# First mixer: items three in flight, operands of 31 and 36 rows padded to 128, gate folded into the scaling, output begun in the last items, gate slot moved

## The chip, the cores and the metric

The kernel runs on one core of a Trainium2 chip. Its metric is the device time of one execution in microseconds (us); lower is better. The core has five engines with queues of their own that work in parallel and wait for each other on semaphores: TensorE (PE: matmuls and transposes into PSUM banks), VectorE (DVE), ScalarE (ACT), GpSimd (POOL) and SyncE (SP, which issues the weight loads).

## The reference

The program is a chain of transformer blocks on 512 tokens of width 1024, in float32. The change touches only the mixer of the first block, whose heart is this:

```python
def _even_mixer(h, w_in, ...):
    aq, ak, av, ao, ai, af, bq, bkc, bvc, bks, bvs, bkw, bvw, bg = _split(h @ w_in, EVEN_SIZES)
    ya = _mlstm(aq, ak, av, ao, ai + a_i_b, af + a_f_b, a_conv, a_norm)
    yb = _nsa(bq, bkc, bvc, bks, bvs, bkw, bvw, bg + b_g_b, b_cmp_pos, b_cmp_w1, b_cmp_w2)
    return jnp.concatenate([ya, yb], -1) @ w_out

# _nsa, for each block of queries, head pair and branch (compressed, selected, window)
    p = _masked_softmax(s, mask)          # s = q k^T; 31 compressed keys, or up to 512
    o = gb[..., 0:1] * o_cmp + gb[..., 1:2] * o_sel + gb[..., 2:3] * o_win

# _mlstm, for each of 4 heads (gates ig, fg; written here over all 512 tokens at once)
    S = (q k^T) * exp(D - m);  hc = (S v) / max(|den|, exp(-m))
    hn = (hs - mean) * rsqrt(var + eps) * norm_g;  ya = hn * sigmoid(o)
```

`_mlstm` is the "memory" part, `_nsa` the "heads" part. Behind the mixer come a residual with layer norm, an MLP and the other blocks, which the change leaves alone.

## The kernel before

Every weight is float32 and is used as a high and a low half. SP loads a slot (up to 128 x 2048) into one of two raw buffers; ScalarE writes the high half (L1293, whi); the low half, raw minus high, is written by GpSimd (L3119, wlo) or VectorE (L2047). A product is three matmuls: whi with the high half of x, wlo with it, whi with x's low half (L591 to L593, `mm3`). There are two pairs of halves: a slot's pair can be written only when the slot two before it has been used. The order of slots is written out in `weight_plan`: e_in (four slots of 256 columns), e_g (96 columns: the gates of both parts), e_vs, the two compressions with e_qk, two more e_qk, e_vo (four) and e_out (eight half slots, four for each half of the columns). All engines' programs go through it in that order.

In the first stage (to about 134 us of the span) TensorE makes the projections. From the gate product, VectorE and ScalarE work out the memory part's row vectors (`r_ls`, `r_b`, `r_M`: bias, Abs, Exp, +1, Ln, two scans; ScalarE L1521 to L1527, VectorE L2385 to L2404), and the window sums for the compression (`windows`, L2374) are VectorE's too. ScalarE's copy `hw` into an_e (L1482 in the records, which is the line of the copy helper) and a transpose of it follow.

From about 134 to 365 us runs a loop over 48 items. An item is a block of 128 queries (q, 0 to 3), two key groups (g), two head pairs (j) and a branch (br: 0 compressed with 31 keys, 1 selected, 2 window with (q + 1) x 128 keys). Its steps are:
- `first`: scores on TensorE (L914 to L916 for br 0, L918 to L920 otherwise), row maxima on VectorE (L2531), exp with row sum on ScalarE (L1617)
- `scaled`, on VectorE: reciprocal of the sums (L2538), times the gate (L2542), for q = 0 and br = 0 times a row mask (L2545), then P times that (L2549), for each of two heads
- `second`: transposes of P on TensorE (L933), the copy to PT on VectorE for odd items (L2292), on ScalarE for even ones (L1482)
- `third`: product with the values (L948; operand vc of 31 rows for br 0, vsw of 128 rows otherwise), and after br 2 the copy to yb (L2576), or for q = 3 its split into xh and xl (ScalarE L1641, VectorE L2572)

Round n of the loop does `first(n)`, one unit of the memory part, `second(n - 1)` and `third(n - 2)` on every engine; on VectorE `scaled(n)` stands behind the unit. From item 12 on every third round does a second unit. P and PT have two copies each, by n % 2. The units are, in order, the rest of e_qk and the e_vo products; for each of four heads four decay units (scores L864, decay with nmr and sel of 36 rows L867, VectorE L2468) and four value units (L877, denominator L1586, L2475, L2477, scaling L2479); then statistics (L2486, L2490), norms (L2500), and transposes of the memory output (L611, copied by L2114). The last unit splits yb of the first three query blocks (L2511). Behind the loop TensorE waits for all of this and begins the output, e_out (L591 again).

Of the kernel before, what the change touches and what calls it, by code (L numbers as in the profile page):

```python
# [7 lines left out]
F = mybir.dt.float32  # L8
# [300 lines left out]
def weight_plan(I):  # L309
# [21 lines left out]
    add_fm("e_in", v, 0, 1024)  # L331
    plan.slot("e_g", v[:, :, 3328:3424])
    add_fm("e_vs", v, 1024, 1280)
# [66 lines left out]
def memory(nc, k):  # L400
# [19 lines left out]
    def even():  # L420
        with ExitStack() as sc:
# [9 lines left out]
            s.gts, s.nmr, s.gcol = tmp("gts", [128, NT, 24]), tmp("nmr", [36, T], R), tmp("gcol", [128, 2, NT, 4])  # L431
            s.sel, s.vc = tmp("sel", [36, 512], R), tmp("vc", [32, 2, 2, 64])
# [5 lines left out]
            s.P, s.PT, s.PT_e = tmp("P", [128, 4, T]), tmp("PT", [128, 4, T]), tmp("PTe", [128, 1280])  # L438
# [5 lines left out]
            s.blk = [x[:, 0:2, :].rearrange("p a (l g m) -> p (a l) g m", l=8, g=2) for x in (s.P, s.PT)]  # L444
# [132 lines left out]
def tensor_program(nc, k):  # L577
# [212 lines left out]
    def even():  # L790
        e = k.even
        fm("e_in", [[("e_in", 2 * n), ("e_in", 2 * n + 1)] for n in range(4)], x, need=lambda kk: ("x", kk))
        pe.wait_ge(at("con"))
# [7 lines left out]
        slots.done()  # L801

# [48 lines left out]
        def memory():  # L851
# [8 lines left out]
            for hh in range(4):  # L860
# [11 lines left out]
                for q in range(NT):  # L872
                    pe.wait_ge(at("PT_e", hh, 3))
# [7 lines left out]
            yield  # L881
            yield
# [6 lines left out]
            yield  # L889
# [33 lines left out]
        def second(n):  # L923
# [3 lines left out]
            for z in range(0, nk, 256):  # L927
                bank = take(("at", n, z))
                for i, kk in enumerate(range(z, min(z + 256, nk), 128)):
                    w = min(128, nk - kk)  # L930
                    for h in range(2):
                        o = i * 256 + h * 128
                        ins = M.transpose(bank[0:w, o:o + 128], e.P[:, (n % 2) * 2 + h, kk:kk + w], ident)  # L933
                ins.then_inc(*made.inc(("made", ("at", n, z)), ("P turned", n)))

        def third(n):
# [7 lines left out]
            for kk in range(0, nk, 128):  # L944
                w = min(128, nk - kk)
                lhs = e.vc[0:31, g, :, :] if br == 0 else e.vsw[:, kk // 128, br - 1, g, :, :]
                rhs = e.PT[0:w, (n % 2) * 2 + kk // 256, kk % 256 * 2:kk % 256 * 2 + 256]
# [5 lines left out]
        for n in range(N + 2):  # L953
# [15 lines left out]
        ho.next("ln")
        tm("e_out", ("e_out",), 0, D, x, early=True, after=residual)  # L970
# [2462 lines left out]
```

## Time and profile before

| | us |
| --- | --- |
| three runs | 3425.53, 3427.07, 3427.49 (median 3427.07) |
| the profiled execution, own time | 3425.47 |
| its span | 3424.2 |
| TensorE busy | 3264.3 (95%) |
| VectorE busy | 2040.2 (60%) |
| ScalarE busy | 1458.4 (43%) |
| GpSimd busy | 915.4 (27%) |

The profile is of one execution. Times in rows are from the span's start. PEld is the weight load of TensorE, which overlaps the matmuls; the ends of matmuls are modelled, so for TensorE the distance from start to start says more than the durations. The granted clock is a share of full speed: 1.00 is 2.4 GHz and 0.50 is 1.2 GHz. What stands in brackets behind a row is the engine's idle time ahead of it and what ended that.

### The profile page before, as it was taken

How to read it: one execution, taken by the hardware profiler on the slowest of the kernel's cores; microseconds unless marked ns; L12 is line 12 of the kernel's file. 1: busy time of each engine (PE TensorE's matmuls, PEld its weight loads, DVE VectorE, ACT ScalarE, POOL GpSimd, SP SyncE). 2: the span in 40 equal slices, each digit the busy share in tenths (PEclk: the TensorE clock that was granted, in tenths of full speed). 3: DMA queues.
4: the chain of work that ended last, by engine and by line, in shares of the span. 5: the costliest groups of instructions: out<-in, count | busy, mean ns of one | idle time of the engine just before them, and what ended most of it. 6: DMA issues, size and time to landing. Idle time of an engine off the chain costs nothing.

```text
span 3424.2 us, 47853 instructions
## 1 busy us (share of the span) xinstructions
PE 3264.3 (95%) x20089; PEld 2885.8 (84%) x20092; DVE 2040.2 (60%) x3066; ACT 1458.4 (43%) x2246; POOL 915.4 (27%) x415
## 2 busy tenths in 40 slices
PE   8898999999879999999999999999999999999998
PEld 6786789988667899979899878999999998789998
DVE  4557555464683644567556635755785566367556
ACT  4454345453432544445334323543453343235433
POOL 3120024321421233311233231223222332312232
PEclk9999999999999999999999999999999999999999
DMA  3310323331112233222332323233323323232232
GB/s 129 102 50 1 111 74 118 105 105 60 52 43 74 82 106 121 93 86 69 123 105 87 111 74 99 84 90 111 111 74 117 105 87 111 74 99 94 90 107 75
DMA packets 239815, 308.97 MB, mean 90 GB/s; under 512 B 8337, under 2 KB 168097, under 8 KB 239089
## 3 DMA queue, kind: packets, MB, share of 16 engines
q1 hardware_dynamic: 236016, 291.41, 26.4%
q0 software_dynamic: 3584, 14.52, 1.2%
q8 instruction: 158, 2.59, 0.3%
q14 instruction: 57, 0.46, 0.0%
HBM read 303.80 MB, written 2.10 MB: 89 GB/s over the span
## 4 chain that ended last, share of the span: by engine, by line
PE 73%; DVE 21%; ACT 4%; issue 2%; DMA 0%; POOL 0%; DVEq 0%; ACTq 0%
PE bank L591 23%; PE bank L593 23%; PE bank L592 23%; DVE wlo L2041 3%; ACT whi L1293 1%; DVE wraw L2063 1%; DVE raw_w L2063 1%; DVE xl L2114 1%; DVE wkk_o L2865 1%; ACT P_e L1617 1%; DVE gb L2862 1%; DVE uv_x L2995 1%; DVE ul_w L2241 1%; DVE P_e L2549 1%; PE bank L1232 1%
## 5 line engine op out<-in xcount | busy, mean ns | idle before, releaser
L3119 POOL TENSOR_TENSOR wlo<-wraw,whi 128x1024 fp32r<-128x1024 f32 (+4 forms) x219 | 565.8, 2587 | 1606.4 <-ACT whi L1293 1605.9
L591 PE MATMUL bank<-xh,whi 128*128 128x256 f32 (+1 forms) x2456 | 722.9, 294 | 48.7 <-DVE zt L2236 21.0
L1293 ACT ACTIVATE whi<-wraw 128x1024 fp32r<-128x1024 f32 (+3 forms) x426 | 440.5, 1038 | 693.7 <-PE bank L593 553.9
L593 PE MATMUL bank<-xh,wlo 128*128 128x256 f32 (+1 forms) x2456 | 717.9, 292 | 0.0
L592 PE MATMUL bank<-xl,whi 128*128 128x256 f32 (+1 forms) x2456 | 714.0, 291 | 0.0
L591 PEld LDWEIGHTS bank<-xh,whi 128*128 128x128 f32 x2456 | 466.2, 190 | 69.4 <-issue 27.6
L3119 POOL TENSOR_TENSOR wlo<-raw_w,whi 128x1024 fp32r<-128x1024 f32 (+1 forms) x130 | 310.1, 2388 | 724.6 <-ACT whi L1293 724.6
L592 PEld LDWEIGHTS bank<-xl,whi 128*128 128x128 f32 x2456 | 466.3, 190 | 10.4
L593 PEld LDWEIGHTS bank<-xh,wlo 128*128 128x128 f32 x2456 | 465.2, 189 | 10.6
L591 PE MATMUL bank<-whi,uh_w 128*128 128x512 f32 x1216 | 473.8, 390 | 0.0
L593 PE MATMUL bank<-whi,ul_w 128*128 128x512 f32 x1216 | 473.3, 389 | 0.0
L592 PE MATMUL bank<-wlo,uh_w 128*128 128x512 f32 x1216 | 473.2, 389 | 0.0
L1293 ACT ACTIVATE whi<-raw_w 128x1024 fp32r<-128x1024 f32 (+1 forms) x315 | 307.8, 979 | 362.3 <-PE bank L593 263.1
L2041 DVE TENSOR_TENSOR wlo<-wraw,whi 128x1024 fp32r<-128x1024 f32 (+1 forms) x207 | 239.8, 1161 | 315.6 <-ACT whi L1293 314.8
L591 PE MATMUL bank<-whi,xh 128*128 128x512 f32 (+2 forms) x976 | 375.7, 385 | 9.0 <-POOL wlo L3119 3.6
L591 PE MATMUL bank<-ah_w,whi 128*128 128x256 f32 x1296 | 367.4, 284 | 10.7 <-DVE wraw L2063 6.8
L592 PE MATMUL bank<-wlo,xh 128*128 128x512 f32 (+2 forms) x976 | 369.8, 379 | 0.0
L593 PE MATMUL bank<-whi,xl 128*128 128x512 f32 (+2 forms) x976 | 369.7, 379 | 0.0
L592 PE MATMUL bank<-al_w,whi 128*128 128x256 f32 x1296 | 366.6, 283 | 0.0
L593 PE MATMUL bank<-ah_w,wlo 128*128 128x256 f32 x1296 | 366.5, 283 | 0.0
L2041 DVE TENSOR_TENSOR wlo<-raw_w,whi 128x1024 fp32r<-128x1024 f32 (+1 forms) x185 | 211.8, 1147 | 253.7 <-ACT whi L1293 252.9
L593 PEld LDWEIGHTS bank<-whi,ul_w 128*128 128x128 f32 x1216 | 228.2, 188 | 48.0
(401 smaller groups left out, 5085.8 us busy)
## 6 DMA issues: line engine op xcount, KB each, us to landing
wraw<-in_w_in SPq DMA_DIRECT2D x26, 1024.0 KB, 5.3
wraw<-in_ffn_w_down SPq DMA_DIRECT2D x20, 1024.0 KB, 5.1
raw_w<-in_ffn_w_down SPq DMA_DIRECT2D x20, 1024.0 KB, 5.1
raw_w<-in_mlp_w SPq DMA_DIRECT2D x19, 1024.0 KB, 5.1
wraw<-in_mlp_w SPq DMA_DIRECT2D x17, 1024.0 KB, 5.1
wraw<-in_ffn_w_gate SPq DMA_DIRECT2D x32, 512.0 KB, 5.1
raw_w<-in_ffn_w_gate SPq DMA_DIRECT2D x32, 512.0 KB, 4.9
raw_w<-in_ffn_w_up SPq DMA_DIRECT2D x32, 512.0 KB, 4.5
```

Source lines behind the costliest of these rows:

```text
L591: M.matmul(o, lh, rh, start=start, stop=False, skip_group_check=more)
L592: M.matmul(o, lh, rl, start=False, stop=False, skip_group_check=more)
L593: return M.matmul(o, ll, rh, start=False, stop=stop, skip_group_check=more)
L1232: i = M.matmul(bank[:, q * 128:(q + 1) * 128], s.PT[:, hh % 2, o:o + 128], s.vt[:, t, hh * 128:(hh + 1) * 128], start=(t == 0), stop=(t == q))
L1293: A.activation(hi, raw, ACT.Copy).then_inc(*k.w_hi.inc(("hi", j)))
L1617: A.activation(e.P[:, (n % 2) * 2 + h, 0:nk], ring.of(key)[:, 0:nk], ACT.Exp, bias=m, accum_out=e.rsum[:, n % 4, h:h + 1]).then_inc(*done. ...
L2041: V.tensor_tensor(lo, raw, hi.bitcast(F), ALU.subtract).then_inc(*k.w_lov.inc(("lo", j)))
L2063: V.tensor_tensor(b, x, y, ALU.subtract).then_inc(*done.inc(("sum of", j)))
L2114: V.tensor_tensor(lo, ring.of((*key, f))[:, :].rearrange("p (f t) -> p f t", f=4), hi.bitcast(F), ALU.subtract).then_inc(*done.inc((*name, ...
L2241: V.tensor_tensor(quarter(s.ul, u, c, a), t.rearrange("p (f t) -> p f t", t=256), quarter(s.uh, u, c, a).bitcast(F), ALU.subtract).then_in ...
L2549: V.tensor_scalar(p, p, c[:, hf:hf + 1], None, ALU.mult).then_inc(*done.inc(("P scaled", n)))
L3119: G.tensor_tensor(lo[:, 0:n], raw[:, 0:n], hi[:, 0:n].bitcast(F), ALU.subtract).then_inc(*k.w_lo.inc(("lo", j)))
```

## The change

It has six parts, all in the first mixer.
1. The gates' slot e_g goes ahead of the last e_in slot, and the row vectors' chain with it on each engine: on VectorE ahead of the last slot's copies, on ScalarE Abs and Exp ahead of them and Ln between them.
2. The loop has one more item in flight: `scaled(n - 1)`, `second(n - 2)`, `third(n - 3)`, N + 3 rounds, P and PT split by branch in place of n % 2. On VectorE `scaled(n - 1)` stands ahead of the unit for items 0 and 1 and behind it from item 2 on. The second unit comes from item 9 on.
3. vc, PT of branch 0, nmr and sel have 128 rows, the added ones zero.
4. The gate is the second pointer operand of L2549's successor; the multiply L2542 goes, and the row mask is applied once to the first gates.
5. Statistics are made in each value unit; value unit q waits for decay unit q only, and the denominator's max takes its second operand as a pointer. There are 61 units where there were 64.
6. The first half of the rows' products of output column 0 (`out_first`, 12 matmuls for each token tile) for tiles 0 and 1 is made in the last two units, for tiles 2 and 3 right behind the loop; `out_second` follows, and then the second half of the columns. The split of yb moves behind the loop on VectorE, and to round N on ScalarE.

```diff
-    add_fm("e_in", v, 0, 1024)
+    add_fm("e_in", v, 0, 768)
     plan.slot("e_g", v[:, :, 3328:3424])
+    add_fm("e_in", v, 768, 1024)
...
-            s.gts, s.nmr, s.gcol = tmp("gts", [128, NT, 24]), tmp("nmr", [36, T], R), tmp("gcol", [128, 2, NT, 4])
-            s.sel, s.vc = tmp("sel", [36, 512], R), tmp("vc", [32, 2, 2, 64])
+            s.gts, s.nmr, s.gcol = tmp("gts", [128, NT, 24]), tmp("nmr", [128, T], R), tmp("gcol", [128, 2, NT, 4])
+            s.sel, s.vc = tmp("sel", [128, 512], R), tmp("vc", [128, 2, 2, 64])
...
-            s.P, s.PT, s.PT_e = tmp("P", [128, 4, T]), tmp("PT", [128, 4, T]), tmp("PTe", [128, 1280])
+            s.P, s.PT, s.PT_e = tmp("P", [128, 2112]), tmp("PT", [128, 2304]), tmp("PTe", [128, 1280])
...
+            s.p_of = [(s.P[:, a:a + w], s.P[:, a + w:a + 2 * w]) for a, w in ((0, 32), (64, 512), (1088, 512))]
+            s.pt_of = [s.PT[:, a:a + w] for a, w in ((0, 256), (256, 1024), (1280, 1024))]
...
# TensorE
...
-        fm("e_in", [[("e_in", 2 * n), ("e_in", 2 * n + 1)] for n in range(4)], x, need=lambda kk: ("x", kk))
-        pe.wait_ge(at("con"))
+        fm("e_in", [[("e_in", 2 * n), ("e_in", 2 * n + 1)] for n in range(3)], x, need=lambda kk: ("x", kk))
...
+        fm("e_in", [[("e_in", 6), ("e_in", 7)]], x)
+        pe.wait_ge(at("con"))
...
-                    pe.wait_ge(at("PT_e", hh, 3))
+                    pe.wait_ge(at("PT_e", hh, q))
...
+                if q > 1:
+                    out_first(q - 2)
...
+        def out_first(tt):
+
+            key = ("e_out", 0, tt)
+            pe.wait_ge(at("og turned", tt))
+            bank = take(key, True)
+            for p, kr in enumerate(k_items(8)[0:2]):
+                tm_part(slots.get("e_out", p), kr, bank, key, tt, x, 8, None, 512, last=tt == NT - 1)
+
+        def out_second():
+            slots.done(2)
+            for kr in k_items(8)[2:4]:
+                j = slots.get("e_out")
+                for tt in range(NT):
+                    key = ("e_out", 0, tt)
+                    if tt < NT - 1:
+                        pe.wait_ge(at("yb split"))
+                    else:
+                        pe.wait_ge(at("yb split 3"))
+                    tm_part(j, kr, ring.of(key), key, tt, x, 8, None, 512, last=tt == NT - 1)
+                    if kr[1] == 8:
+                        ring.drop(key)
+                slots.done()
 
         pe.wait_ge(at("cmb"))
...
-                lhs = e.vc[0:31, g, :, :] if br == 0 else e.vsw[:, kk // 128, br - 1, g, :, :]
-                rhs = e.PT[0:w, (n % 2) * 2 + kk // 256, kk % 256 * 2:kk % 256 * 2 + 256]
+                lhs = e.vc[:, g, :, :] if br == 0 else e.vsw[:, kk // 128, br - 1, g, :, :]
+                rhs = e.pt_of[br][:, kk * 2:kk * 2 + 256]
...
-        for n in range(N + 2):
+        for n in range(N + 3):
             if n < N:
                 first(n)
             next(units, None)
-            if n >= 12 and n % 3 == 0:
+            if n >= 9 and n % 3 == 0:
                 next(units, None)
-            if 0 <= n - 1 < N:
-                second(n - 1)
             if 0 <= n - 2 < N:
-                third(n - 2)
+                second(n - 2)
+            if 0 <= n - 3 < N:
+                third(n - 3)
         run(units)
         made.so_far(("end", "even", "pe"))
...
+        out_first(2)
+        out_first(3)
+        out_second()
+        tm("e_out", ("e_out",), 512, D, x, early=True, after=residual)
...
# ScalarE
...
+        def e_in_ln(key):
+            e_in(key)
+            if key[1] == 6:
+                act.wait_ge(at("r_ls one"))
+                A.activation(e.r_ls, e.r_ls, ACT.Ln).then_inc(*done.inc(("r_ls ln",)))
+        fm("e_in", [[("e_in", 6), ("e_in", 7)]], e_in_ln)
+        act.wait_ge(at("con"))
+        act.wait_ge(at("eps"))
+        def e_vs(key, tt):
+            copy_out(key, e.vsw[:, tt, :, :, 0, :], ring.of(key)[:, 0:256].rearrange("p (a g d) -> p a g d", a=2, g=2), ("vsw one", tt))
+        run(tm_units("e_vs", ("e_vs",), e_vs))
         act.wait_ge(at("r_bM"))
...
+            if n == N:
+                act.wait_ge(at("yb one", 35))
+                act.wait_ge(at("yb", 35))
+                A.activation(xh[:, 4:8, 0:384], e.yb[:, :, 0:384], ACT.Copy).then_inc(*done.inc(("yb hi",)))
...
# VectorE
...
+        V.memset(e.vc[:, :, :, :], 0.0).then_inc(*done.inc(("vc empty",)))
...
-        fm("e_in", [[("e_in", 6), ("e_in", 7)]], e_in)
-        windows(1)
...
+        windows(1)
...
+        fm("e_in", [[("e_in", 6), ("e_in", 7)]], e_in)
...
+        first_gate = e.gts[:, 0, :].rearrange("p (h j) -> p h j", j=3)[:, :, 0]
+        V.tensor_scalar(first_gate, first_gate, con[:, C_ROW:C_ROW + 1], None, ALU.mult).then_inc(*done.inc(("gts masked",)))
+        dve.wait_ge(at("gts masked"))
...
-                    V.tensor_tensor(d, d, e.gcol[:, 1, q, hh:hh + 1], ALU.max).then_inc(*done.inc())
+                    V.tensor_scalar(d, d, e.gcol[:, 1, q, hh:hh + 1], None, ALU.max).then_inc(*done.inc())
                     dve.wait_ge(done.now())
...
-                    yield
-            for q in range(NT):
-                for hh in range(4):
-                    j = q * 4 + hh
                     dve.wait_ge(at("hs", hh, q))
                     V.bn_stats(st[:, j, 0, :], e.hs[:, q, hh, :]).then_inc(*done.inc())
-                dve.wait_ge(done.now())
-                for hh in range(4):
-                    j = q * 4 + hh
+                    dve.wait_ge(done.now())
...
-            V.reciprocal(c, c).then_inc(*done.inc())
             h0 = 4 * g + 2 * j
             gate = e.gts[:, q, :].rearrange("p (h j) -> p h j", j=3)[:, h0:h0 + 2, br]
+            V.reciprocal(c, c).then_inc(*done.inc())
             dve.wait_ge(done.now())
-            V.tensor_tensor(c, c, gate, ALU.mult).then_inc(*done.inc())
-            dve.wait_ge(done.now())
-            if br == 0 and q == 0:
-                V.tensor_scalar(c, c, con[:, C_ROW:C_ROW + 1], None, ALU.mult).then_inc(*done.inc())
-                dve.wait_ge(done.now())
             for hf in range(2):
-                p = e.P[:, (n % 2) * 2 + hf, 0:nk]
-                V.tensor_scalar(p, p, c[:, hf:hf + 1], None, ALU.mult).then_inc(*done.inc(("P scaled", n)))
+                p = e.p_of[br][hf][:, 0:nk]
+                V.tensor_scalar(p, p, c[:, hf:hf + 1], gate[:, hf:hf + 1], ALU.mult, ALU.mult).then_inc(*done.inc(("P scaled", n)))
 
         def second(n):
...
-        for n in range(N + 2):
+        for n in range(N + 3):
             if n < N:
                 first(n)
+            if 0 <= n - 1 < 2:
+                scaled(n - 1)
             next(units, None)
-            if n < N:
-                scaled(n)
-            if n >= 12 and n % 3 == 0:
+            if 2 <= n - 1 < N:
+                scaled(n - 1)
+            if n >= 9 and n % 3 == 0:
                 next(units, None)
-            if 0 <= n - 1 < N:
-                second(n - 1)
             if 0 <= n - 2 < N:
-                third(n - 2)
+                second(n - 2)
+            if 0 <= n - 3 < N:
+                third(n - 3)
         run(units)
+        dve.wait_ge(at("yb hi"))
+        hi, lo = xh[:, 4:8, 0:384], xl[:, 4:8, 0:384]
+        V.tensor_tensor(lo, e.yb[:, :, 0:384], hi.bitcast(F), ALU.subtract).then_inc(*done.inc(("yb split",)))
         barrier("even")
         enter()
         ho.next("ln")
```

In ScalarE's program the waits for buffers go from the item two before to the item three before, and its loop changes as TensorE's does.

## Rows read from the trace of the kernel before

**Rows 1.** page, section 4: the chain that ended last, share of the span by engine
```profile
PE 73%; DVE 21%; ACT 4%; issue 2%; DMA 0%; POOL 0%; DVEq 0%; ACTq 0%
```

**Rows 2.** windows, five stretches of the first mixer; columns as in the first line
```profile
core 0: us, PE busy (x) PEld busy (x) DVE busy (x) ACT busy (x) POOL busy (x), PEclk, DMA share, GB/s
65.50:110.00 44.50, 35.26 (x226) 31.56 (x226) 27.25 (x32) 17.13 (x22) 11.24 (x7) 0.92 0.24 79
155.70:219.70 64.00, 63.79 (x498) 60.72 (x497) 28.99 (x98) 40.62 (x96) 14.11 (x4) 0.96 0.18 58
219.70:300.10 80.40, 72.77 (x409) 52.53 (x407) 54.41 (x194) 36.78 (x132) 4.87 (x2) 0.96 0.04 14
300.10:364.90 64.80, 50.77 (x267) 38.41 (x267) 50.87 (x166) 27.95 (x81) 0.77 (x1) 0.89 0.09 33
364.90:410.00 45.10, 45.10 (x202) 36.61 (x203) 19.91 (x27) 10.82 (x15) 5.84 (x4) 1.00 0.36 117
```

**Rows 3.** windows, for the granted clock (PEclk), four stretches; same columns
```profile
95.90:99.30 3.40, 3.40 (x13) 2.80 (x12) 0.20 (x2) 1.35 (x2) 0.00 (x0) 0.51 0.00 0
154.00:160.00 6.00, 6.00 (x25) 5.02 (x26) 2.57 (x14) 4.92 (x12) 0.00 (x0) 0.50 0.50 167
322.85:341.85 19.00, 13.18 (x55) 9.72 (x54) 15.89 (x56) 9.63 (x24) 0.00 (x0) 0.73 0.00 0
250.95:300.10 49.15, 44.84 (x264) 32.61 (x263) 34.36 (x122) 21.83 (x82) 0.00 (x0) 1.00 0.00 1
```

**Rows 4.** timeline of TensorE: start us, us, instruction [idle before <-releaser]
```profile
69.19 0.58 PE L591 MATMUL bank<-whi,xh 128*128 128x256 f32 x1 [3.65 <-POOL wlo L3119]
...
95.37 0.27 PE L825 MATMUL bank<-con,an_e 64*128 64x64 f32 x1 [3.50 <-ACT an_e L1482]
...
153.97 0.69 PE L933 MATMUL bank<-con,P_e 128*128 128x128 f32 x2 [3.48 <-DVE P_e L2549]
```

**Rows 5.** timeline of ScalarE and GpSimd around the gate slot
```profile
48.84 0.60 ACT L1482 ACTIVATE kvT_e<-bank 128x512 f32<-128x512 f32 x1 [5.00 <-PE bank L593]
...
64.37 4.77 POOL L3119 TENSOR_TENSOR wlo<-wraw,whi 128x2048 fp32r<-128x2048 f32 x1 [12.08 <-ACT whi L1293]
...
91.51 0.63 ACT L1527 ACTIVATE gb<-og_e 4x512 f32<-4x512 f32 x1 [4.60 <-DVE og_e L2404]
```

**Rows 6.** timeline of ScalarE behind the exp of item 2
```profile
156.28 0.63 ACT L1537 ACTIVATE qk_e<-PTe_e 128x512 f32<-128x512 f32 x1
```

**Rows 7.** waits in 219.7 to 364.9: total us, times, longest
```profile
ACT P_e L1617 <- DVE nm_e L2531: 73.1, 32, 3.6
DVE PTe_e L2468 <- ACT kvT_e L1482: 14.5, 12, 1.4
...
DVE den_e L2475 <- ACT den_e L1586: 9.8, 12, 1.0
```

**Rows 8.** timeline of TensorE, an item's last product and the next item's first
```profile
165.76 0.60 PE L948 MATMUL bank<-PT_e,vsw_e 128*128 128x256 f32 x2
166.01 0.41 PE L918 MATMUL bank<-kh_e,qs_e 128*128 128x128 f32 x1
...
169.94 0.69 PE L948 MATMUL bank<-PT_e,vc_e 31*128 31x256 f32 x2
170.56 0.28 PE L914 MATMUL bank<-kch_e,qs_e 128*128 128x32 f32 x1
```

**Rows 9.** VectorE by form, from 130 or 219.7 on: count, busy us, mean ns, idle
```profile
L2549 DVE TENSOR_SCALAR P_e<-P_e,rsum_e 128x128 f32<-128x128 f32 x16 | 3.9, 283 | 0.3
...
L2542 DVE TENSOR_TENSOR rsum_e<-rsum_e,gts_e 128x2 f32<-128x2 f32 x33 | 5.3, 161 | 1.1
...
L2500 DVE TENSOR_SCALAR qk_e<-qk_e,mv,rs 128x128 f32<-128x128 f32 x16 | 4.4, 342 | 0.1
...
L2486 DVE BATCH_NORM_STATS2 st<-qk_e 128x6 f32<-128x128 f32 x16 | 3.4, 277 | 0.0
...
L2490 DVE BATCH_NORM_AGGREGATE mv<-st 128x2 f32<-128x6 f32 x16 | 1.5, 158 | 0.1
```

More of the change, by code:

```diff
@@ L880, in memory @@
             yield
-            yield
-            yield
             for q in range(NT):
@@ L1505, in e_in @@
                     A.activation(e.kh[other, i - 6, g, :], src, ACT.Copy).then_inc(*done.inc(("ks hi twice", i - 6, g)))
-        fm("e_in", [[("e_in", 2 * n), ("e_in", 2 * n + 1)] for n in range(4)], e_in)
-        act.wait_ge(at("con"))
-        act.wait_ge(at("eps"))
+        fm("e_in", [[("e_in", 2 * n), ("e_in", 2 * n + 1)] for n in range(3)], e_in)
         slots.get("e_g")
@@ L1516, in even @@
         A.activation(e.r_f, bank[64:68, :], ACT.Copy).then_inc(*done.inc(("r_f",), ("free", ("e_g",))))
-        def e_vs(key, tt):
-            copy_out(key, e.vsw[:, tt, :, :, 0, :], ring.of(key)[:, 0:256].rearrange("p (a g d) -> p a g d", a=2, g=2), ("vsw one", tt))
-        run(tm_units("e_vs", ("e_vs",), e_vs))
+        slots.prepare()
         act.wait_ge(at("r_f bias"))
@@ L1523, in even @@
         A.activation(e.r_ls, e.r_ls, ACT.Exp, scale=-1.0).then_inc(*done.inc(("r_ls exp",)))
-        act.wait_ge(at("r_ls one"))
-        A.activation(e.r_ls, e.r_ls, ACT.Ln).then_inc(*done.inc(("r_ls ln",)))
+        def e_in_ln(key):
[9 more added lines that the diff above has]
+        run(tm_units("e_vs", ("e_vs",), e_vs))
         act.wait_ge(at("r_bM"))
@@ L1597, in memory @@
                 yield
-            act.wait_ge(at("yb one", 35))
-            act.wait_ge(at("yb", 35))
-            A.activation(xh[:, 4:8, 0:384], e.yb[:, :, 0:384], ACT.Copy).then_inc(*done.inc(("yb hi",)))
-            yield
         units = memory()
@@ L2354, in even @@
         V.tensor_copy(k.idb[:, :], k.ident)
-        V.tensor_copy(e.sel[:, :], con[0:36, C_SEL:C_SEL + 512]).then_inc(*done.inc(("sel",)))
+        V.tensor_copy(e.sel[:, :], con[:, C_SEL:C_SEL + 512]).then_inc(*done.inc(("sel",)))
         V.memset(e.nmr[:, :].bitcast(F), 0.0).then_inc(*done.inc(("nmr empty",)))
@@ L2508, in memory @@
                 yield
-            dve.wait_ge(at("yb hi"))
-            hi, lo = xh[:, 4:8, 0:384], xl[:, 4:8, 0:384]
-            V.tensor_tensor(lo, e.yb[:, :, 0:384], hi.bitcast(F), ALU.subtract).then_inc(*done.inc(("yb split",)))
-            yield
         units = memory()
@@ L2518, in even @@
         dve.wait_ge(at("made", key))
+        dve.wait_ge(at("vc empty"))
         V.tensor_copy(e.vc[0:31, :, 0, :], src)
@@ L2576, in third @@
                 V.tensor_copy(e.yb[64:128, f, s], o[64:128, 128:256]).then_inc(*done.inc(("yb", n), ("free", key)))
-        for n in range(N + 2):
+        for n in range(N + 3):
             if n < N:
                 first(n)
+            if 0 <= n - 1 < 2:
+                scaled(n - 1)
             next(units, None)
-            if n < N:
-                scaled(n)
-            if n >= 12 and n % 3 == 0:
+            if 2 <= n - 1 < N:
+                scaled(n - 1)
+            if n >= 9 and n % 3 == 0:
                 next(units, None)
-            if 0 <= n - 1 < N:
-                second(n - 1)
             if 0 <= n - 2 < N:
-                third(n - 2)
+                second(n - 2)
+            if 0 <= n - 3 < N:
+                third(n - 3)
         run(units)
+        dve.wait_ge(at("yb hi"))
+        hi, lo = xh[:, 4:8, 0:384], xl[:, 4:8, 0:384]
+        V.tensor_tensor(lo, e.yb[:, :, 0:384], hi.bitcast(F), ALU.subtract).then_inc(*done.inc(("yb split",)))
         barrier("even")
@@ L3167, in even @@
         G.dma_start(e.w2, I["w2"]).then_inc(*k.landed["w2"].inc(("w2",)))
-        slots.skip("e_in", 4)
+        slots.skip("e_in", 3)
         slots.skip("e_g", 1)
+        slots.skip("e_in", 1)
         slots.get("e_vs")
```

33 lines of the change are left out of this document (11 added, 22 removed).

## The prediction

> **What bounds the kernel now.** I began with the chain that ended last [rows 1]: 73% of it runs on TensorE, and of the rest most on VectorE. So time can be taken out only where TensorE waits or is slow. The table of stretches [rows 2] says where, in the first mixer: in 65.5 to 110 TensorE is busy 35.26 of 44.5 us; in 155.7 to 219.7 it is full (63.79 of 64); in 219.7 to 300.1 it is busy 72.77 of 80.4; in 300.1 to 364.9 only 50.77 of 64.8; in 364.9 to 410 it is full again, 202 matmuls in 45.1 us, 0.223 us each. These five stretches have different limits, and the change touches all of them. The granted clock [rows 3] is at its lower level (1.2 GHz, shown as 0.50) for the 3.4 us from 95.9 and in 154 to 160, both times right behind a wait of 3.5 us [rows 4]. TensorE's waits there are 3.65 us for a weight's low half from GpSimd (at 69.19), 3.50 us for ScalarE's hw (L1482, out an_e), and 3.48 us for item 0's scaled P. A stretch of 3.4 us at half clock costs 1.7 us where TensorE is the limit.
>
> In 219.7 to 364.9 the waits [rows 7] read otherwise: ScalarE's exp waits 73.1 us for the row maxima of VectorE, and VectorE waits 14.5 + 9.8 = 24.3 us for ScalarE in its memory units (decay and denominator). TensorE and GpSimd set little there: the bound is a loop, VectorE max, ScalarE exp, ScalarE unit, VectorE unit, VectorE scaling, next max.
>
> **A, gate slot moved (base 48.8 us).** Now the e_g product ends at 65.5 and the gate rows are the first thing behind it, with the next high part just before; its low half on GpSimd takes 4.77 us [rows 5], so TensorE waits 3.65 us, and 1.7 more go at half clock. After the change the last e_in slot, 48 matmuls, lies between the gate product and e_vs, so the split of e_vs and the gate chain, which ends with ScalarE's L1527 at 91.51 [rows 5], have 11 us more. That removes 3.65 + 1.7 and 3.50 + 1.7 = 10.55 us. In return the last e_in slot's own pair can be split only when the slot two before it is used, at 48.8. With some 2 us for the high half (an estimate, under half of GpSimd's 4.77 for the same size) behind the copy that starts at 48.84, and 4.77 for the low half, it is ready at about 56.0. The gate product, 24 matmuls of 0.223, started at 48.8 ends at 54.2. So a new wait of 1.8 us. Sum -8.7. Bounds: the new wait may grow to 3.5 with a fall of the clock (-5.5), or vanish (-10.5). The gate chain is queued on VectorE ahead of the last two e_in copies and the window sums; it holds the low half of the next DVE-split slot, which I price at 0 to 2.
>
> **B, three in flight, items 0 to 3.** TensorE stands at 153.97 for P of item 0 [rows 4]. A lag of one more item asks for it later; scaling of items 0 and 1 stays ahead of the unit. But what then comes next is PT(0), copied by ScalarE behind its table load and a silu that ends at 156.9 [rows 6]: about 157.0, against third(0)'s 154.59 now. So only part of 3.48 + 1.7 us goes: -2.5 (0 to -4.5).
>
> **C, padding.** The trace has the same product with 128 rows and 31 rows [rows 8]: from start to next start it is 0.25 us with 128 (165.76 to 166.01) and 0.62 with 31 (169.94 to 170.56): 0.37 us per such item. Five of the 16 fall where TensorE is full (items 3 to 15), -1.9; the extra unit from item 9 on moves work into it, +0.8. Sum -1.1 (-3 to +1). In the rest TensorE has slack, and padding nets nothing there. A rule speaks against it: the Trainium skill, page "TensorE: Matmul & The Clock Gate", section "Why this matters for your kernels", says that a single K=32 matmul takes the same time as K=128, with which the padding would gain 0 and C would be +0.8. The trace disagrees with 0.25 against 0.62.
>
> **D, items 16 to 35, VectorE's loop.** Per item the gate multiply (L2542) goes: 0.161 plus 0.035 of spacing, 0.196. The scaling gets a second pointer: L2500 (two) at 128x128 took 342 ns, L2549 (one) 283 [rows 9]; +0.057 each, two per item, +0.11. Net -0.085 x 20 = -1.7. The statistics move into the value units: 0.277 + 0.158, with one more signal wait between them and one for hs 0.52 (an estimate), and the max with a pointer +0.07. Twelve of the 16 units lie here (the other four begin after 305): 12 x 0.59 = +7.1. Unit shift, -0.5. Sum +4.9 (+2 to +7). The depth doesn't take the 24.3 us of waits for ScalarE, in my reading: after the change the scaling of the item before stands behind the unit, the unit waits for ScalarE's unit, and this for exp(n) and that for max(n); the loop stays closed.
>
> **E, item 36 to the output's first matmul, 64.8 us.** Out go 16 statistics and 16 aggregates in four batches, 1.20 each, -4.8; in come four inline at 0.6, +2.4; scaling -0.085 x 12 = -1.0; the last wait for the yb split -1.0, as the two output tiles left stand ahead of it; one more lap in flight at the end, +1.7. Sum -2.7. And two first halves of output tiles, 24 matmuls, are done inside, where TensorE idles 14 of 64.8 us: 24 x 0.223 [rows 2] = -5.4. The clock is 0.89 there; more work in it could be at half speed, +0.8. Sum -7.3 (-11 to -2). Weights for both e_out slots are on the chip before, since DMA moves little there (33 GB/s, [rows 2]).
>
> **Sum.** -8.7 - 2.5 - 1.1 + 4.9 - 7.3 = -14.7 on the profiled execution's 3425.47 (its span is 3424.2, 1.3 less), 3410.8; the median shown is 1.6 higher, so 3412 us. What follows (the output stage and the MLP) is bound by TensorE at 45.1 of 45.1, so the gain carries through to the end. Of the moved slot everything moves: its load on SP's queue changes place with the last e_in slot's, its high half on ScalarE's and its low half on GpSimd's. No wait of TensorE there is for a load [rows 4], and DMA is busy 0.24 of the stretch behind, so I price the loads at nothing; without that cover one slot's load would be in question.
>
> **Rivals.** Four cases, the main one being the sum above.
>
> R2: the depth does open the loop. ScalarE's exp no longer feeds the scaling in its own round, and were the 24.3 us of waits in VectorE's units gone for half or more, with D at -9 instead of +4.9, the sum is -29, 3398. For: the waits, 24.3 us in all, are the largest of VectorE's [rows 7]. Against: the order of the unit ahead of the scaling.
>
> R3: only the small parts count. New wait of A with a fallen clock and the low half queued behind the gate chain (-4), B nothing, E -4, D +5: -5, 3422.
>
> R4, on the other side: the clock. In 322.85 to 341.85 TensorE is busy 13.18 of 19 us and the clock is 0.73 [rows 3]: where it works in short bursts between waits, it is slow part of the time. In 250.95 to 300.1 it is busy 44.84 of 49.15 us at clock 1.00. Should the changed order of bursts bring the lower level there too, at a mean clock of 0.60 its work takes 44.84 / 0.60 = 74.7 us, and TensorE takes the bound over: +25.6 on the sum of the others, -14.7, gives 3438. It decides, slower by more than 6.9 us, once the clock's mean there falls below 0.63, where 44.84 us of work become 71. For: padding and the moved unit shorten TensorE's work in the same loop, so it idles a larger share. Against: the change takes 0.37 us of matmul from every third item there, of 44.84 in all, and the stretch now holds 1.00. The Trainium skill, page "TensorE: Matmul & The Clock Gate", section "A second HAM failure mode: psum-queue depth-cycling", describes a kernel whose engine idled briefly between groups of matmuls and so kept falling back; the trace agrees for 322.85 to 341.85 (0.73), while 250.95 to 300.1 has waits too and stays at 1.00.
>
> **How the numbers follow.** Main case 0.62, its own range -24 to -6 (3403 to 3421), from the bounds above taken partly together; R2 0.17; R3 0.12; R4 0.09. A measurement of this kernel can tell 0.2%, 6.9 us, from no change. Most of R3 (0.10) and a tenth of the main case (0.06) lie within it: 0.16. Slower is R4 but for a little, 0.08. Faster is the rest, 0.76. The range to leave out no more than 2 in 10: 3396 to 3424, the upper end the small case, the lower end the open loop.
>
> **What would show it.** After: no wait of over 2 us for GpSimd or hw between 50 and 110, one of about 1.8 at the slot behind the gates (A); no L948 with 31 rows, and about 0.25 us from it to the next first (C); L2549 at 0.34 for 128 columns and 0.56 for 512 (D); VectorE still waiting some 20 us for ScalarE's kvT and den between items 16 and 35 (against R2); the clock above 0.9 there (against R4); 24 matmuls of the output ahead of the last third (E). It is wrong if the loop in D opens, if ScalarE, which the moved Exp and Ln give other table loads, becomes late in A, or if a stall in another place lowers the clock.

## The result and the profile after

The changed kernel took 3414.23 us (median of 6 runs, 3413.44 to 3415.14), the kernel before 3426.34 us (6 runs): a ratio of 0.9963, 95% interval 0.9951 to 0.9974, so 12.1 us less where the forecast had 14.7. The profiled execution took 3413.44 us, its span 3412.1.

The windows of the changed kernel, cut where item 0, item 4, item 16 and item 36 begin, where the output begins behind the loop, and where the MLP's first product begins (columns as in [rows 2]):

```profile
126.20:149.20 23.00, 20.61 (x128) 17.85 (x126) 14.60 (x32) 17.40 (x27) 6.87 (x2) 0.99 0.29 92
149.20:208.80 59.60, 58.23 (x463) 55.82 (x462) 26.21 (x73) 39.30 (x94) 13.92 (x4) 0.98 0.17 54
208.80:293.70 84.90, 68.14 (x397) 53.92 (x395) 59.63 (x194) 37.61 (x129) 4.66 (x2) 0.92 0.04 13
293.70:357.80 64.10, 51.85 (x307) 40.99 (x306) 48.09 (x134) 28.77 (x84) 0.77 (x1) 1.00 0.10 33
357.80:399.00 41.20, 41.20 (x187) 33.45 (x186) 23.80 (x32) 11.88 (x17) 5.82 (x4) 1.00 0.40 132
```

The same points in both traces, from the starts of TensorE's instructions, give the balance by stage:

| to | before, at us | after, at us | this stage | forecast |
| --- | --- | --- | --- | --- |
| item 0 | 134.35 | 126.23 | -8.1 | A -8.7 |
| item 4 | 161.9 | 149.2 | -4.6 | B -2.5 |
| item 16 | 219.7 | 208.8 | +1.8 | C -1.1 |
| item 36 | 298.1 | 293.7 | +6.5 | D +4.9 |
| the MLP's first matmul | 411.5 | 399.0 | -8.1 | E -7.3 |
| end of the span | 3424.2 | 3412.1 | +0.4 | 0 |

The sum is -12.1. Items 16 to 35 became slower by 6.5 us, in a kernel that is faster by 12.1. TensorE's longer waits in the timeline of the changed kernel, with what ended them:

```profile
55.05 0.51 PE L594 MATMUL bank<-xh,whi 128*128 128x512 f32 x1 [1.84 <-POOL wlo L3141]
...
101.67 0.47 PE L594 MATMUL bank<-xh,whi 128*128 128x512 f32 x1 [2.07 <-DVE wlo L2075]
...
108.60 0.27 PE L829 MATMUL bank<-con,an_e 64*128 64x64 f32 x1 [1.12 <-ACT an_e L1506]
...
148.57 1.17 PE L973 MATMUL bank<-PT_e,vc_e 128*128 128x256 f32 x2 [1.96 <-ACT PT_e L1506]
...
216.20 0.45 PE L959 MATMUL bank<-con,P_e 128*128 128x128 f32 x1 [3.40 <-DVE PTe_e L2500]
...
230.62 0.41 PE L959 MATMUL bank<-con,P_e 128*31 128x128 f32 x2 [1.72 <-DVE P_e L2566]
...
253.61 0.41 PE L959 MATMUL bank<-con,P_e 128*31 128x128 f32 x2 [1.62 <-DVE P_e L2566]
...
271.05 0.33 PE L871 MATMUL bank<-nmr_e,sel_e 128*128 128x128 f32 x1 [1.72 <-DVE gb L2593]
```

Against [rows 4], 3.65 us became 1.84 (forecast 1.8) in another place, 3.50 became 1.12, and item 0's 3.48 became 1.96. The last is no longer a wait for the scaling but for ScalarE's copy of PT, which is what step B named as late next. The wait of 2.07 us for VectorE's low half is no new one. The kernel before has it too, later and with 3.4 us of half clock behind it, which the changed kernel's trace doesn't have there (granted clock 1.00 in its window):

```profile
109.42 0.61 PE L591 MATMUL bank<-xh,whi 128*128 128x512 f32 x1 [2.08 <-DVE wlo L2047]
...
109.80:113.20 3.40, 3.40 (x10) 2.67 (x9) 0.00 (x0) 0.52 (x1) 0.00 (x0) 0.53 1.08 356
...
101.60:105.10 3.50, 3.43 (x15) 2.83 (x16) 0.00 (x0) 0.05 (x1) 0.00 (x0) 1.00 1.07 348
```

The first two lines are of the kernel before, the third of the changed one. The longest wait, 3.40 us at 216.20, is for a decay unit of VectorE behind the last e_vo products. And the waits between item 16 and the output, answering to [rows 7]:

```profile
ACT P_e L1641 <- DVE nm_e L2553: 77.5, 32, 4.8
...
DVE PTe_e L2500 <- ACT kvT_e L1506: 13.1, 12, 1.3
...
PE bank L959 <- DVE P_e L2566: 10.6, 12, 1.7
DVE den_e L2507 <- ACT den_e L1616: 9.8, 12, 1.0
```

VectorE's waits for ScalarE are 22.9 us where they were 24.3: with a third item in flight and the old order they are nearly as they were. The scaling with two pointers and the statistics, by form, answer to [rows 9]:

```profile
L2566 DVE TENSOR_SCALAR P_e<-P_e,rsum_e,gts_e 128x31 f32<-128x31 f32 x32 | 8.1, 296 | 0.6
...
L2566 DVE TENSOR_SCALAR P_e<-P_e,rsum_e,gts_e 128x512 f32<-128x512 f32 x16 | 8.0, 543 | 0.3
...
L2514 DVE BATCH_NORM_STATS2 st<-qk_e 128x6 f32<-128x128 f32 x16 | 4.7, 294 | 0.6
L2507 DVE TENSOR_SCALAR den_e<-den_e,gcol_e 128x1 f32<-128x1 f32 x16 | 3.4, 212 | 9.8 <-ACT den_e L1616 9.8
L2516 DVE BATCH_NORM_AGGREGATE mv<-st 128x2 f32<-128x6 f32 x16 | 2.9, 182 | 0.5
```

With 128 rows the compressed product passes at once to the next item, as the timeline of TensorE shows (0.24 us from start to start, against 0.62 in [rows 8]):

```profile
162.47 0.60 PE L973 MATMUL bank<-PT_e,vc_e 128*128 128x256 f32 x2
162.71 0.41 PE L944 MATMUL bank<-kh_e,qs_e 128*128 128x128 f32 x1
```

### The profile page after: what moved, and what is told of

It reads as the page before. It is cut to its first block, busy times and chain, and to the rows that moved or that the text cites. A ratio compares the mean times of both kernels' runs of the same rounds, so it can differ in the third digit from the quotient of the medians.

```text
span 3412.1 us, 47807 instructions
## 1 busy us (share of the span) xinstructions
PE 3250.6 (95%) x20089; PEld 2882.8 (84%) x20092; DVE 2044.4 (60%) x3016; ACT 1461.8 (43%) x2248; POOL 916.4 (27%) x415
## 4 chain that ended last, share of the span: by engine, by line
PE 75%; DVE 19%; ACT 4%; issue 2%; DMA 0%; POOL 0%; DVEq 0%; ACTq 0%
PE bank L594 24%; PE bank L596 23%; PE bank L595 23%; DVE wlo L2069 3%; ACT whi L1317 1%; DVE wraw L2091 1%; ACT P_e L1641 1%; DVE xl L2142 1%; DVE raw_w L2091 1%; DVE wkk_o L2887 1%; DVE gb L2884 1%; DVE P_e L2566 1%; PE bank L614 1%; PE bank L1256 1%; PE bank L1247 1%
## 5 line engine op out<-in xcount | busy, mean ns | idle before, releaser
L3141 POOL TENSOR_TENSOR wlo<-wraw,whi 128x1024 fp32r<-128x1024 f32 (+3 forms) x219 | 565.3, 2584 | 1586.8 <-ACT whi L1317 1586.3
L595 PEld LDWEIGHTS bank<-xl,whi 128*128 128x128 f32 x2456 | 467.2, 190 | 10.2
```

The lines of the kernel that those rows point to most:

```text
L595: M.matmul(o, lh, rl, start=False, stop=False, skip_group_check=more)
L3141: G.tensor_tensor(lo[:, 0:n], raw[:, 0:n], hi[:, 0:n].bitcast(F), ALU.subtract).then_inc(*k.w_lo.inc(("lo", j)))
```

## The experiments

Each was timed beside the kernel before (medians 3426.4 to 3427.2 in these sessions). The interval is that of the ratio to the kernel before; differences between variants are differences of medians.

**gate_slot_only: part A alone, on the kernel before.**

```diff
-    add_fm("e_in", v, 0, 1024)
+    add_fm("e_in", v, 0, 768)
     plan.slot("e_g", v[:, :, 3328:3424])
+    add_fm("e_in", v, 768, 1024)
```

with the order on every engine's queue as in the change.

> The kernel before with the gate slot moved and nothing else. If part A stands by itself, two waits of TensorE (3.65 and 3.50 us) with their half-clock stretches go and one of about 1.8 us with its own comes, and item 0 starts 7.6 to 8.7 us earlier: 3426.3 - 8 = 3418, if nothing later gives it back. Rival: the stall at item 0's scaled P is bound by VectorE and ScalarE, not by when TensorE gets there, so it grows by what TensorE gained: 3422 to 3424.

Measured: 3419.01 us (11 runs, 3416.95 to 3423.27), ratio 0.9979 (0.997 to 0.9987): -7.7. Item 0 starts at 126.1, as in the changed kernel, and in the medians nearly all of it arrives. The rival falls: the wait at item 0 is as long as before, not longer, and begins 8 us earlier. It is in TensorE's timeline:

```profile
145.70 0.69 PE L935 MATMUL bank<-con,P_e 128*128 128x128 f32 x2 [3.48 <-DVE P_e L2557]
```

**scale_first: every scaling ahead of the unit.** On the changed kernel, VectorE's loop:

```diff
-            if 0 <= n - 1 < 2:
+            if 0 <= n - 1 < N:
                 scaled(n - 1)
             next(units, None)
-            if 2 <= n - 1 < N:
-                scaled(n - 1)
```

> The changed kernel with the scaling of item n - 1 ahead of the unit for all items, not for items 0 and 1 alone. Theory: VectorE's 22.9 us of waits for ScalarE in items 16 on (13.1 for the decay, 9.8 for the denominator) stand there because the scaling is behind the unit; ahead of it, it fills them: at least 10 us of the 22.9 go, 3414.2 - 10 to - 15 = 3399 to 3404. Rival: the waits go and come back as waits of ScalarE or TensorE, because the units' low halves and copies come later by the scaling's 0.5 to 1.2 us in the items where TensorE is full: 3412 to 3418.

Measured: 3390.29 us (4 runs, 3390.02 to 3395.88), ratio 0.9898 (0.9884 to 0.9911): 23.9 us below the changed kernel, more than the theory asked for. The waits of this kernel from 209 to 350 us, and its windows (items 16 to 35, then to the end of the loop):

```profile
ACT P_e L1641 <- DVE nm_e L2553: 56.5, 32, 4.8
...
DVE PTe_e L2500 <- ACT kvT_e L1506: 3.8, 8, 0.7
```

```profile
208.50:278.80 70.30, 63.62 (x397) 51.06 (x395) 59.05 (x194) 37.61 (x131) 4.66 (x2) 0.95 0.05 16
278.80:337.40 58.60, 51.90 (x306) 41.65 (x305) 47.20 (x132) 28.62 (x83) 0.77 (x1) 0.97 0.10 36
```

Item 16 begins at 208.5 against 208.8 in the changed kernel, item 36 at 278.8 against 293.7, the output's product at 337.7 against 357.85. So up to item 16, where TensorE is full, the order is worth little, and the next twenty items are 14.6 us shorter. VectorE does the same work in them, 59.05 us of 70.3 where it was 59.63 of 84.9. (This profiled execution was the slowest of its four runs, 3395.88; in it 2.7 of the 20.2 us are given back behind the mixer.) Its wait for kvT fell from 13.1 to 3.8, and that for den from 9.8 to 1.1. One round of each shows where it went. The changed kernel's VectorE, by its timeline:

```profile
298.85 0.21 DVE L2507 TENSOR_SCALAR den_e<-den_e,gcol_e 128x1 f32<-128x1 f32 x1
...
300.10 1.25 DVE L2553 TENSOR_REDUCE nm_e<-bank 128x1 f32<-128x512 f32 x2
302.33 0.21 DVE L2507 TENSOR_SCALAR den_e<-den_e,gcol_e 128x1 f32<-128x1 f32 x1 [0.98 <-ACT den_e L1616]
```

and scale_first's:

```profile
285.17 0.21 DVE L2507 TENSOR_SCALAR den_e<-den_e,gcol_e 128x1 f32<-128x1 f32 x1 [0.36 <-ACT den_e L1616]
...
287.34 1.28 DVE L2553 TENSOR_REDUCE nm_e<-bank 128x1 f32<-128x512 f32 x2
288.54 0.15 DVE L2562 RECIPROCAL rsum_e<-rsum_e 128x2 f32<-128x2 f32 x1
```

Behind the maxima VectorE now goes on with the scaling at once (288.54), and ScalarE makes the exp and its unit meanwhile.

**depth_two and scale_first_two: the depth, with either order.** Both have `second(n - 1)` and `third(n - 2)` on the three engines:

```diff
             if 0 <= n - 2 < N:
-                second(n - 2)
-            if 0 <= n - 3 < N:
-                third(n - 3)
+                third(n - 2)
```

with `second(n - 1)` ahead of it. depth_two has `scaled(n)` behind the unit, scale_first_two `scaled(n - 1)` ahead of it.

> The changed kernel with only two items in flight: scaled(n) behind the unit, second(n - 1), third(n - 2), as in the kernel before; all else as changed. Theory: depth pays only where item 0 to 4 stood (4.6 us in the trace) and a little at the end: 3417 to 3420. Rival 1: depth also carried the last items, where output work fills TensorE: 3422 or more. Rival 2: depth gave nothing, and the 4.6 us came from the earlier start: 3414.

Measured: 3416.56 us (7 runs, 3414.79 to 3420.81 but for one at 8197), ratio 0.9971 (0.996 to 0.9983). Against the changed kernel +2.3: a little less than the theory's, and the end of its range is not told from the second rival's 3414. The stall at item 0 is back (TensorE waits 3.40 us for P at 145.72) and item 4 begins at 153.2, not 149.2. The output's first product begins at 362.35, 4.5 us behind the changed kernel's, so what depth gives in items 0 to 4 lasts through the loop; the two traces end 3.1 us apart, the medians 2.3.

> The kernel with every scaling ahead of the unit (3390.3 measured), with second and third one round earlier, so two items in flight for the transposes and products, and scaled(n - 1) as there. Theory: what opened the loop is that the scaling no longer waits for the exp of its own round and stands where VectorE waited; the third item in flight adds only the stall of item 0 to 4: 3392 to 3397. Rival: TensorE's transposes then stand behind VectorE's scaling of the same round, so the depth is what carries it: 3402 or more.

Measured: 3418.11 us (11 runs, 3412.62 to 3422.8), ratio 0.9976 (0.9967 to 0.9984). The theory fell and the rival held. The four corners:

| | scaling behind the unit | scaling ahead of it |
| --- | --- | --- |
| two in flight | 3416.6 | 3418.1 |
| three in flight | 3414.2 | 3390.3 |

Neither is worth much alone; together they are worth 26 us. The waits of scale_first_two, from 209 to 350 us, say why:

```profile
PE bank L959 <- DVE P_e L2566: 28.6, 26, 3.7
...
DVE nm_e L2553 <- PE bank L946: 9.9, 8, 4.6
```

Here VectorE's waits for ScalarE have gone too (kvT 4.1 us), but TensorE's transposes now wait for the scaling that VectorE does in the same round, 28.6 us, and VectorE for the scores behind them, 9.9. One closed loop was opened and another closed. With the third item in flight TensorE takes P of the round before.

**stats_batched: part 5's statistics undone.** Statistics in four batches of four in two units of their own, as before:

> The changed kernel with the statistics in batches of four again, in two units of their own. Theory: inline they cost VectorE some 0.53 us per value unit, 8.5 in all, and in batches 4.8, so items 16 to 35 gain about 6.5 us and the last items lose 4.8 or so: 3411 to 3413. Rival: in the last items the batches stand in the loop where nothing hides them while inline they partly filled waits: 3416 to 3419.

Measured: 3412.72 us (5 runs, 3411.21 to 3414.53), ratio 0.9961 (0.9947 to 0.9974). 1.5 us below the changed kernel, on the side of the theory but with runs that overlap. The trace shows where the cost moves. Items 16 to 35 take 78.7 us (item 16 begins at 209.85, item 36 at 288.57) where the changed kernel needs 84.9, and from there to the output it is 69.65 us against 64.15: -6.1 and +5.5, close to the theory's -6.5 and +4.8. Inline statistics cost in one stage nearly what they save in the other.

**out_behind: no output in the last units.**

```diff
-                if q > 1:
-                    out_first(q - 2)
...
+        for tt in range(NT):
+            out_first(tt)
```

> The changed kernel with the first halves of all four output tiles behind the loop, none in its last units. Term E holds 24 matmuls, 5.4 us (in the changed kernel's trace the two groups took 3.0 and 3.0 us in 337.0 to 343.3), moved into TensorE's idle time: without it 3414.2 + 5.4 to 6 = 3420. Rival: in that place they lengthen the loop, since the items' maxima wait behind them: 3414 to 3417.

Measured: 3417.95 us (8 runs, 3416.27 to 3421.46), ratio 0.9976 (0.9965 to 0.9986): +3.7, between the two. The output's product begins at 355.8 here and at 357.85 in the changed kernel, so the 24 matmuls lengthen the loop by 2.05 us and take 24 x 0.223 = 5.4 from behind it: a net 3.3 of the 3.7.

**rows_31: the padding undone in the matmuls.**

```diff
-                lhs = e.vc[:, g, :, :] if br == 0 else ...
-                rhs = e.pt_of[br][:, kk * 2:kk * 2 + 256]
+                lhs = e.vc[0:31, g, :, :] if br == 0 else ...
+                rhs = e.pt_of[br][0:w, kk * 2:kk * 2 + 256]
```

and nmr and sel cut to 36 rows.

> The changed kernel with the operands cut to their 31 and 36 rows again in the matmuls (vc, PT, nmr, sel), all else as changed. Theory of the forecast: 0.37 us for each item of branch 0 comes back where TensorE is full, five of them and a few more: +2 to +3, 3416.5. Rival 1, that rows don't matter: 3414.2. Rival 2, each of the 16 items and 16 decay units counts in full, 0.37 and 0.35: +11, 3425.

Measured: 3420.51 us (11 runs, 3416.07 to 3422.47), ratio 0.9981 (0.9972 to 0.999): +6.3, which is three times the forecast's price and between theory and second rival. Its trace shows TensorE at half clock where the changed kernel has it too (around items 0 and 16), and from 250 us on in five stretches where the changed kernel has two. These are the two longest of the five, with TensorE busy all of them:

```profile
274.50:280.50 6.00, 6.00 (x23) 4.41 (x22) 4.16 (x14) 2.28 (x7) 0.00 (x0) 0.50 0.00 0
328.50:335.50 7.00, 7.00 (x25) 5.08 (x25) 5.49 (x14) 2.66 (x7) 0.00 (x0) 0.52 0.00 0
```

How the 6.3 us divide between rows and clock is not settled: this profiled execution was the fastest of its runs (3416.07) and ends only 2.6 us behind the changed kernel's. In it item 0 begins 1.3 us later, where no padded operand has been used yet; items 4 to 15 take 1.2 us more, items 16 to 35 0.6 us more, and the rest of the loop 1.3 us more. The decay units lose by short rows as well, which the forecast left out: undisturbed, one of 512 columns takes 1.44 us from its first score matmul to the next instruction with 36 rows (from 208.73 here) and 1.16 with 128 (from 206.99 in the changed kernel).

**gate_mult: the gate multiplied apart.**

```diff
+            V.tensor_tensor(c, c, gate, ALU.mult).then_inc(*done.inc())
+            dve.wait_ge(done.now())
...
-                V.tensor_scalar(p, p, c[:, hf:hf + 1], gate[:, hf:hf + 1], ALU.mult, ALU.mult)
+                V.tensor_scalar(p, p, c[:, hf:hf + 1], None, ALU.mult)
```

> The changed kernel with the gate multiplied into the row sums by an instruction of its own and one pointer in the scaling. VectorE's work grows by 0.196 - 2 x 0.059 = 0.08 us per item, 32 items in VectorE's loop: +2.5, 3416.7. Rival: no part of it is on the path (3414.2), since VectorE waits for ScalarE in the same round; or, as the wait on the reciprocal lengthens, +5.

Measured: 3415.1 us (6 runs, 3413.26 to 3420.57), ratio 0.9969 (0.9958 to 0.9981). No difference in the medians that can be told from the changed kernel. In the traces items 16 to 35 take 86.1 us against 84.9 and the output's first product begins 2.2 us later, so inside the mixer the theory's price is there; 1.6 us of it are not in the whole execution's time.

**On top of scale_first: what each part is worth in the open loop.** The same edits again, with every scaling ahead of the unit.

> Three in flight with every scaling ahead of the unit (3390.3 measured), and the statistics in batches again. There VectorE is busy 59.05 of 70.3 us in items 16 to 35 and stands close to full, so what inline statistics cost it more than batches (8.5 against 4.8 us, an estimate from their rows) should count now: 3386 to 3388. Rival: as behind the unit, where batching moved 3414.2 to 3412.7 only, 1 to 2 us or nothing: 3388 to 3391.

Measured: 3395.25 us, but its four runs lie from 3389.55 to 3398.69, ratio 0.9902 (0.9886 to 0.9918). The medians tell nothing, and the forecast's 3386 to 3388 isn't reached by any run. The trace does tell: items 16 to 35 take 65.6 us where scale_first has 70.3, and the rest of the loop 63.2 where it has 58.9. Batches gain 4.7 us and give 4.3 back.

> Three in flight, every scaling ahead of the unit, operands of 31 and 36 rows in the matmuls. With the scaling behind the unit the short rows cost 6.3 us in the medians (3420.5 against 3414.2). If that was TensorE's own time, as TensorE is busy 63.62 of 70.3 us in items 16 to 35 here, it costs at least as much: 3396 to 3400. Rival: it came from the half-clock stretches that the kernel with short rows showed more of (18.8 against 10.2 us lost in its trace), which depend on where waits fall: anywhere from 3390 to 3396.

Measured: 3397.48 us (5 runs, 3395.57 to 3398.02), ratio 0.9908 (0.9894 to 0.9922): +7.2 in the medians, as the theory had it. But the two traces, 3398.02 and scale_first's slowest run 3395.88, are only 2.1 us apart, and 1.7 more were lost to the clock in the one with short rows (one minus the granted clock, summed over 40 to 420 us: 10.2 against 8.5). By stage, items 4 to 15 cost 1.5 us more, items 16 to 35 nothing (70.2 against 70.3), and the rest of the loop 2.4 us more, with 3.4 us more lost to the clock in it. The cause that the theory gives for items 16 to 35 is not in this trace, and where the medians' 7.2 us arise is not shown.

> Three in flight, every scaling ahead of the unit, the gate as an instruction of its own. Behind the unit it cost 0.9 us in the medians, under what can be told. With VectorE's waits for ScalarE gone its own work sets the rounds, and 0.08 us for each of 32 items should show: +2.5, 3392.8. Rival: no difference that can be told, 3390.3.

Measured: 3393.73 us (4 runs, 3392.62 to 3394.03), ratio 0.9899 (0.9885 to 0.9913): +3.4, near the theory's 2.5, though one of the four runs of scale_first itself lies higher (3395.88). From item 0 to the output's first product the traces have 211.0 against 210.0 us.

> Of the change only the moved gate slot and three in flight, with every scaling ahead of the unit: short rows, gate multiplied apart, statistics in batches, output behind the loop. Theory: depth and order carry most: 3390.3 plus the parts one by one as measured behind the unit (rows 6.3, output 3.7, gate 0.9, statistics -1.5), 9.4 in all: 3400. Rival: the parts need each other, as depth and order did: 3408 or more.

Measured: 3403.88 us (5 runs, 3402.09 to 3404.88), ratio 0.9928 (0.9916 to 0.9941). The theory's 3400 is missed by 4 and the rival's 3408 by 4. The moved slot with depth and order is 23 us of the 36 that scale_first takes off the kernel before; the other parts together are 13.6 where their sizes behind the unit add up to 9.4. The two traces are 6.6 us apart, since the one of scale_first is of its slowest run.

The starts in the traces, in us, beside the time of the profiled execution. The first stage alone differs by 1.6 us between traces whose edits don't touch it: where item 0 begins at 126.7 or later, TensorE had a wait of 1.3 us at 83 to 84 and its half clock behind the wait at 102, not behind the one at 55.

| | item 0 | item 16 | item 36 | output | whole |
| --- | --- | --- | --- | --- | --- |
| changed kernel | 126.2 | 208.8 | 293.7 | 357.9 | 3413.4 |
| stats_batched | 127.4 | 209.9 | 288.6 | 358.2 | 3412.2 |
| rows_31 | 127.5 | 211.3 | 296.8 | 362.2 | 3416.1 |
| gate_mult | 126.3 | 209.1 | 295.2 | 360.1 | 3414.1 |
| scale_first | 127.7 | 208.5 | 278.8 | 337.7 | 3395.9 |
| scale_first_batched | 126.1 | 207.0 | 272.5 | 335.7 | 3389.6 |
| scale_first_rows31 | 127.0 | 209.6 | 279.7 | 341.0 | 3398.0 |
| scale_first_gate_mult | 126.7 | 207.5 | 277.6 | 337.6 | 3393.9 |
| order_alone | 127.8 | 210.3 | 279.9 | 341.3 | 3402.4 |

## Why the prediction was right, point by point

The forecast was -14.7 and -12.1 was measured; the main case came, and none of its rivals. The sum is better than some of its terms: B came out too small, C and D too favourable, and inside A things not counted cancel.

**A, right, in part by luck.** The two waits went, a new one of 1.84 us came at the slot behind the gates where 1.8 was worked out, with a fall of the clock (1.7 us) that only the bound had. The wait for an_e shrank to 1.12 us and didn't vanish. Against these the third wait of the stage, 2.08 us for VectorE's low half, which the forecast didn't name, lost its half clock (-1.7). -8.7 + 1.7 + 1.1 - 1.7 = -7.6 by these rows; -8.1 in the trace, -7.7 in the medians of gate_slot_only.

**B, right in mechanism, too small.** The scaling stopped being the wait and ScalarE's copy of PT became it; the first product of item 0 begins at 148.57 where 157.0 less A's 8.1, 148.9, was worked out. The term of the sum that was mis-sized is the clock: 1.7 us was taken for the stretch behind 153.97, but [rows 3] have it at half clock from 154 to 160, which costs about twice that, and the changed kernel's is 3.4 us long (mean clock 0.52 from 148.8 to 152.2). -4.6 in the traces against -2.5. depth_two shows 4.0 of it as depth; its median is 2.3 above the changed kernel's.

**C, wrong in sign.** The 0.37 us per item is there (0.62 became 0.24), but only four items of branch 0 have their product in this stretch, -1.5. The extra unit of round 9 shifts the order and adds no projection: both traces have 336 matmuls of 128x256 here, 14 units, and what the changed kernel has more is one decay unit, 206.99 to 208.15, +1.2 where 0.8 was put. Two things were not in the term. What is left of item 0's half clock lies behind item 4, 3.0 us of it, +1.5; and TensorE idles 1.4 us in this stretch, where it idled 0.2 (1.10 us of it at 198.26, for scaled P), +1.2. Against it, with one more item in flight some products and transposes of item 13 fall behind the stretch, some -0.5 (an estimate from their distances of 0.1 to 0.12 us). By this +1.9, and +1.8 in the traces. The sentence "In the rest TensorE has slack, and padding nets nothing there" stays open. The medians speak against it: undone, the padding cost 6.3 us, and 7.2 in the open loop, near the 6.1 us that sixteen items of 0.38 make. The traces speak for it in items 16 to 35 (+0.6 and -0.1 us by short rows). Behind item 36 they have +1.3 and +2.4 us, together with more half clock.

**D, right.** +6.5 against +4.9. One value unit of VectorE took 0.66 us from its start to the next instruction before (305.78 to 306.44 in that trace) and takes 1.25 now (298.85 to 300.10 above), the 0.59 of the forecast. The second pointer costs 58 ns at 31 columns and 42 at 512, and the max with a pointer 54 ns where 70 was said. Undone in the traces, the statistics take 6.1 us off this stretch (stats_batched) and without the gate's part it is 1.2 longer (gate_mult): +6.1 - 1.2 is the 4.9 of the forecast. The 1.6 above that can be clock: the mean granted clock of these items fell from 0.96 to 0.92, since 13.6 us at the lower level stand here, where the kernel before has one stretch of 6.8. The claim that carried the forecast, that depth leaves VectorE's waits for ScalarE because the scaling stands behind the unit, is shown by scale_first: the same depth with the other order takes 23.9 us off.

**E, right.** -8.1 against -7.3. Of it the output's matmuls are 3.3 to 3.7 (out_behind), not 5.4, since they aren't wholly hidden; the rest of the loop gave more than 2.7, also because the clock there is 1.00 now, 0.89 before [rows 2].

**The rivals.** R2, that depth opens the loop, did not happen, but its mechanism exists: it wants the order too. R3's low end stood on B giving nothing; its terms as listed, -4, 0, -4 and +5, add up to -3 and not to the -5 written (-4 with C). R4's fall of the clock came in three stretches between items 16 and 35, 6.8 us from 213.8 and twice 3.4; the mean there is 0.92, and R4 wanted it below 0.63.

## What to carry to other kernels

Where two engines hand work back and forth within one round, deeper buffering alone buys little (2.3 us here) as long as one engine's queue has, between its two halves of the hand-over, an item that waits for the other engine; and reordering alone moves the wait to the third engine (+1.5 us here). Try depth and order together, and read after each which wait took the place of the one removed. Where medians are a few microseconds apart, look in the traces for the stage in which the difference arises: batches of statistics, 1.5 us in the medians, are -6.1 and +5.5 us in two stages, while the 7.2 us of the short rows appear in no stage that was thought to hold them.

## What the runs showed of the hardware that was not expected

TensorE's clock fell (to 0.50, its lower level, 1.2 GHz) behind waits of 1.62 us (at 253.6) and 1.72 us (at 271.05) in the changed kernel and did not behind one of 1.72 us (at 230.6) in the same trace. Behind the first two it had some 3.4 us at the lower level, as the second and third window show. The first window is the longest stretch of this trace at the lower level; it begins behind a wait of 1.72 us (at 212.29) and holds the wait of 3.40 us at 216.20:

```profile
213.80:220.60 6.80, 4.40 (x17) 3.85 (x17) 5.28 (x14) 2.94 (x9) 0.53 (x1) 0.52 0.47 154
254.20:257.70 3.50, 3.50 (x15) 3.17 (x16) 2.43 (x9) 1.71 (x7) 0.00 (x0) 0.54 0.00 0
271.20:274.50 3.30, 3.30 (x16) 2.81 (x16) 2.28 (x10) 1.84 (x8) 0.00 (x0) 0.55 0.00 0
```

The same wait at the same place differs from trace to trace as well. Behind VectorE's low half, 2.07 to 2.08 us, the clock fell in the kernel before and in scale_first (0.50 in 103.8 to 107.2) and stayed at 1.00 in the changed kernel and in gate_mult. Behind GpSimd's, 1.82 to 1.86 us, it fell in the changed kernel and stayed at 1.00 in scale_first and gate_mult. So the length of the last wait doesn't tell alone. The Trainium skill, page "TensorE: Matmul & The Clock Gate", section "A second HAM failure mode: psum-queue depth-cycling", has brief idle times between groups of matmuls bring the lower level; the trace agrees in these places, and has the same idle time without it in another.

Some variants also spread more from run to run than others: 3412.62 to 3422.8 us over 11 runs of scale_first_two, 3413.44 to 3415.14 over 6 of the changed kernel. What sets that stays open.
